# A transformer-block kernel: the norm's shift and scale in two parts, two projections split by rows between their slabs, routing steps six then four

## The chip, the core and the metric

One core of a Trainium2 chip runs the whole program. The time is device microseconds (us) of one execution; lower is better. Everything is float32. The engines are PE (TensorE), DVE (VectorE), ACT (ScalarE), POOL (GpSimd) and SP (SyncE, which here only issues transfers).

## What is computed

Two layers on 256 tokens of 1024 features. Only the first part of the first layer is touched by the change, and the routing of its expert layer:

```python
mod = (silu(c) @ w_mod + b_mod)              # 1024 -> 6144
sh1, sc1, gt1, sh2, sc2, gt2 = split(mod, 6)
h = rmsnorm(x, ln_mix_g) * (1 + sc1) + sh1   # 256 x 1024
proj = h @ w_in                              # q, kc, vc, ks, vs, kw, vw, gates, 3 x conv
# attention (compressed, selected, window) and a short convolution, then
x = x + gt1 * (mixed @ w_out)
h2 = rmsnorm(x, ln_ffn_g) * (1 + sc2) + sh2
# 8 heads: scores against 2 x 128 keys, top 16 of each half, top 16 of the 256 sums
x = x + gt2 * sum(g * gelu(h2 . u[expert]) * v[expert])   # 128 experts a token
# then a second layer (block attention, gated delta rule, 3 branches)
```

## The kernel before

**Stages.** 0 to 182 us of the profile are the front: modulation, norm, projections, attention of the first 128 tokens, output projection, first routing. 182 to about 975 us are the expert loop: 128 steps `p`, each of two gathers (`fetch`, POOL, an indirect DMA of 128 rows of `in_puv`, 1 MB), two dot products (`dot`, DVE, L1722), weights (`weight`, ACT) and two accumulations (`accumulate`, PE, L1095). The rest of the attention, the routing of later heads and the second layer are laid between these steps by `loop_chores`. After it comes the end of the second layer.

**Slabs.** A weight matrix is read in slabs of 8 x 128 rows x 512 columns (2 MB, two transfers of 4 x 128 rows each: L2529). The table `SLABS` (L157) numbers them; `W` has four slots and slab `i` of the first 22 goes to slot `i % 4`. `load(i, *free)` in `sync` (L2524) waits for the event that frees the slot and issues; SP does its loads strictly in the order written (from L2540), so one waiting load holds all behind it. The slabs of the front:

- 0 to 3: the columns of `w_mod` for shift and scale of the first norm (`sh1` in 0 and 1, `sc1` in 2 and 3; each slab has 512 of the 1024 features);
- 4 (`S_Q`) queries, 7 (`S_KV`) compressed and selected keys and values, 9 (`S_KW`) window keys, values and gates, 11, 14, 16 (`S_CV`) the convolution's three projections;
- 5, 6, 8, 10, 12, 13, 15, 17 (`S_MOD`) the other eight slabs of `w_mod`, which DVE alone multiplies: `mods(m)`, by `weighted_rows` (L1399), eight DVE instructions of 128 x 512 that sum `w[k] * c[k]` over k;
- 18, 19 (`S_WO`) and 20, 21 (`S_WQ`): output projection and the queries of the routing.

**The first modulation.** For slabs 0 to 3 the work is shared: PE multiplies the first 256 columns (`mod_front`, L806, 8 matmuls, one output row, copied by ACT in `mod_row`), DVE sums the other 256 (`weighted_rows` into `half_buf`, 128 x 256). `columns` (L799) turns the rows into columns of `modc` by single-column matmuls. `mod1` adds the bias and makes `sc1`. Only then do `evacuate` on DVE (L1429; features k = 0, 1, 4, 5) and on ACT (L2159; k = 2, 3, 6, 7) write the normed, scaled, shifted `hT` from the transposes of `norm_T` (L820). `queries` and `keys_values` (matmuls by `feat`, L771, and `token`, L779) run over all eight k for each output tile.

**The order after it.** PE: `flip_bias` (L849), `window`, `conv_project(0, 0)`, `scores_mm(0)` (L937), `compress(0)`, `scores_mm(1)`, ..., `cmp_s1(0)` (L899), ..., `cmp_turn(0, 0)` (L921). DVE: `mods(0)`, `mods(1)`, `blocks` (L1441), `flip_bias` (L1448), `mods(2)`, `mods(3)`, `scores_add(0)` (L1459 and on), `weigh(0)`, `scores_add(1)`, `weigh(1)`, `mods(4)`, `mods(5)`, `compress_k`, `compress_v`, `mods(6)`, `cmp_s2(0)`, `cmp_s3(0)`, ... SP, around there: slab 12 after `mods(2)`, 14 after `mods(3)`, 16 after `mods(4)`, 15 after `conv_project(0, 1)`, 17 after `mods(5)`.

**The routing.** `route(a)` is a generator of small DVE steps: eight or more per head. `loop_chores` lets it advance by a fixed number of steps after each `p` (L495), besides what a gather needs at once:

```python
            while (a, (2 * m + g) // 16) not in idx:
                advance(routes, 1)
...
        advance(routes, 6 if p < 8 else 5 if p < 16 else 4 if p < 33 else 8)
```

`take_i` (L1705) writes the gather indices of two heads; those of heads 2 and 3 are needed from p = 16 on. A gather also needs a free buffer, and in these steps six are in use, so the gathers of `p` wait for the accumulations of `p - 3`.

## Time and profile before

| what | value |
|---|---|
| median of 3 runs | 1257.31 us (1254.69 to 1258.04) |
| the profiled execution | 1260.68 us, its span 1258.9 us |
| PE, DVE, ACT, POOL busy | 1078.0, 796.0, 456.8, 295.8 us |
| moved by DMA | 432.08 MB, mean 343 GB/s |
| granted PE clock, mean | 0.944 of full |

The span is what the profiler saw from first to last instruction; 1.8 us of the execution's own time lie outside. The page of the profile gives the span in 40 slices of 31.5 us; a timeline row is start, length, engine, source line, operation, output and inputs, shape, count, and in brackets the idle time before it with the engine and line that ended it. A matmul in float32 leaves two PE records, so x16 are 8 matmuls.

### The profile page before, as it was taken

The page shows a single profiled execution, that of the slowest core. Times are in us where ns is not written, and L with a number is a line of the kernel's source. Part 1 is how long each engine was busy: PE and PEld are TensorE (multiplying, and loading weights), DVE is VectorE, ACT ScalarE, POOL GpSimd, SP SyncE. Part 2 cuts the span into 40 slices and gives each one's busy share as a digit, 9 for nine tenths or more (in the row PEclk, how much of TensorE's full clock was granted, in tenths as well). Part 3 has the DMA queues.
Part 4 walks back from the last instruction along what each step waited for, and adds up shares of the span by engine and source line. Part 5 has one row for each costly group of instructions (what it writes and reads, how often), then busy time and mean ns, then how long its engine had stood idle before and what let it go on. Part 6 is the DMA issues. An engine that isn't in the chain of part 4 may idle for free.

```text
span 1258.9 us, 13841 instructions
## 1 busy us (share of the span) xinstructions
PE 1078.0 (86%) x5002; PEld 536.8 (43%) x5002; DVE 796.0 (63%) x1865; ACT 456.8 (36%) x1257; POOL 295.8 (23%) x261
## 2 busy tenths in 40 slices
PE   6998986977887676769988789968998998999998
PEld 2887572432343222313332344423443444565543
DVE  5567758887763999764457667576655477645201
ACT  1132127555342444443353343434334423332201
POOL 0000013434343344433323333332323000000000
PEclk9999987998898889989999899988999999999999
DMA  9987419999999999999999999999999975344573
GB/s 388 409 328 316 169 47 370 364 354 411 421 383 421 417 404 395 378 423 401 421 421 420 421 421 420 420 422 363 421 420 423 380 268 200 142 160 154 212 293 127
DMA packets 63487, 432.08 MB, mean 343 GB/s; under 512 B 6931, under 2 KB 10300, under 8 KB 11836
## 3 DMA queue, kind: packets, MB, share of 16 engines
q0 software_dynamic: 36864, 268.45, 52.4%
q1 hardware_dynamic: 26160, 161.76, 32.3%
q10 hardware_dynamic: 396, 0.99, 0.2%
q8 instruction: 39, 0.64, 0.2%
q14 instruction: 28, 0.23, 0.0%
HBM read 430.12 MB, written 1.06 MB: 343 GB/s over the span
## 4 chain that ended last, share of the span: by engine, by line
PE 51%; DVE 20%; DMA 19%; ACT 5%; issue 2%; POOL 1%; another core or an unknown queue 0%; SPq 0%; DVEq 0%
PE ps L1140 22%; DMA AR<-in_puv,idx 17%; PE ps L1095 10%; DVE AR L1722 7%; PE ps L771 4%; PE ps L1254 3%; PE ps L990 2%; DMA W<-in_w_mod 2%; PE ps L1121 1%; PE ps L806 1%; POOL AR L2513 1%; PE ps L1035 1%; ACT av L2258 1%; DVE RT L1694 1%; ACT acc L2137 1%
## 5 line engine op out<-in xcount | busy, mean ns | idle before, releaser
L2513 POOL DMA_INDIRECT AR<-in_puv,idx x256 | 295.5, 1154 | 675.4 <-PE ps L1095 433.1
L1095 PE MATMUL ps<-AR,acc 128*64 128x512 f32 x904 | 286.6, 672 | 100.2 <-ACT acc L2137 98.4
L1722 DVE CUSTOM_DVE_ANT_0 AR<-AR,mixT 128x1024 f32<-128x1024 f32 x128 | 153.5, 1222 | 69.6 <-DMA AR<-in_puv,idx 69.3
L1140 PE MATMUL ps<-W,AR 128*128 128x512 f32 x416 | 189.2, 598 | 0.7 <-ACT AR L2137 0.7
L1095 PEld LDWEIGHTS ps<-AR,acc 128*64 128x64 f32 x904 | 71.8, 146 | 263.8 <-ACT acc L2137 169.5
L1722 DVE CUSTOM_DVE_ANT_0 AR<-AR,tok 128x1024 f32<-128x1024 f32 x128 | 153.0, 1220 | 48.4 <-DMA AR<-in_puv,idx 48.3
L1140 PE MATMUL ps<-W,hT 128*128 128x512 f32 x320 | 158.4, 626 | 6.5 <-DVE PT L2029 5.2
L2256 ACT ACTIVATE av<-av 128x1 f32<-128x1 f32 x256 | 51.3, 200 | 286.7 <-DVE av L1722 286.1
L1140 PEld LDWEIGHTS ps<-W,AR 128*128 128x128 f32 x416 | 76.1, 191 | 78.8 <-issue 76.7
L1140 PEld LDWEIGHTS ps<-W,hT 128*128 128x128 f32 x320 | 58.1, 198 | 83.3 <-issue 74.7
L2137 ACT ACTIVATE acc<-fold,av 128x64 f32<-128x64 f32 x226 | 78.6, 348 | 7.4
L2258 ACT ACTIVATE av<-av,gwp 128x1 f32<-128x1 f32 x256 | 75.4, 294 | 8.3
L771 PE MATMUL ps<-hT,W 128*128 128x256 f32 x320 | 71.4, 383 | 0.0
L771 PEld LDWEIGHTS ps<-hT,W 128*128 128x128 f32 x320 | 61.0, 192 | 8.7 <-issue 0.5
L1095 PE MATMUL ps<-AR,mixT 128*64 128x512 f32 x120 | 47.1, 732 | 17.4 <-ACT mixT L2137 16.8
L2137 ACT ACTIVATE AR<-ps 128x512 f32<-128x512 f32 (+3 forms) x26 | 14.4, 560 | 100.9 <-PE ps L771 43.2
L2007 DVE TENSOR_TENSOR RT<-RT,ps 64x256 f32<-64x256 f32 (+1 forms) x63 | 27.2, 431 | 34.9 <-PE ps L1254 31.4
L2137 ACT ACTIVATE mixT<-ps 128x512 f32<-128x512 f32 (+2 forms) x19 | 9.2, 485 | 81.6 <-PE ps L1140 26.8
L2256 ACT ACT_TABLE_LOAD x26 | 33.4, 1283 | 0.5
L1035 PEld LDWEIGHTS ps<-hT,W 128*128 128x128 f32 x224 | 27.6, 202 | 9.6 <-issue 9.5
L1140 PE MATMUL ps<-W,tok 128*128 128x512 f32 x64 | 31.3, 625 | 0.0
L1035 PE MATMUL ps<-hT,W 128*128 128x128 f32 x224 | 30.0, 291 | 0.0
(459 smaller groups left out, 1311.2 us busy)
## 6 DMA issues: line engine op xcount, KB each, us to landing
W<-in_w_in SPq DMA_DIRECT2D x90, 1024.0 KB, 11.5
W<-in_w_mod SPq DMA_DIRECT2D x24, 1024.0 KB, 16.0
W<-in_wba SPq DMA_DIRECT2D x8, 1024.0 KB
W<-in_wbb SPq DMA_DIRECT2D x8, 1024.0 KB
W<-in_wo SPq DMA_DIRECT2D x8, 1024.0 KB
W<-in_w_out SPq DMA_DIRECT2D x4, 1024.0 KB, 5.7
W<-in_wq SPq DMA_DIRECT2D x4, 1024.0 KB
AR<-in_puv,idx POOLq DMA_INDIRECT x256
```

The source lines that it names most:

```text
L771: t = mm(b[:, o:o + S], slab(i)[:, k, c:c + P], src[:, k, :], start=(k == 0), stop=(k == 7))
L990: t = mm(b[:, :], mixT[:, k, a * P:a * P + P], slab(S_WO[n])[:, k, :], start=(k == 0), stop=(k == 7))
L1035: t = mm(b[:, j * P:j * P + P], slab(S_WQ[m // 2])[:, k, c:c + P], hT[:, k, a * P:a * P + P], start=(k == 0), stop=(k == 7))
L1095: t = mm(of(("E", a, c))[64 * g:64 * g + 64, :], dg_at((2 * p + g) % NDG, late), GB[:, places[g], D + c * 512:D + c * 512 + 512], start=(m ...
L1140: t = mm(b[:, :], src[:, k, :], slab(i)[:, k, :], start=(k == 0), stop=(k == 7))
L1254: t = mm(b[c, q * P + c.start:q * P + c.stop], lhsT[c, q, c], rhs[c, q, c], start=True, stop=True)
L1722: ttr(GB[:, n, 0:D], GB[:, n, 0:D], H2[a][g], 1.0, 0.0, MUL, ADD, av[:, a, c:c + 1]).then_inc(*ve.sig("dot", p, g))
L2007: t = tt(o[c, :, c], o[c, :, c], src[c, :, c], SUB)
L2137: act(dst, src, ACT.Copy, **how).then_inc(*ac.sig(*name))
L2256: t = link(act(w, w, ACT.Gelu_apprx_tanh))
L2258: t = link(act(w, w, ACT.Copy, scale=gwp[:, a, c:c + 1]))
L2513: eng.indirect_dma_start(GB[:, n, :], None, puv, bass.IndirectOffsetOnAxis(ap=idx[:, a, c:c + 1], axis=0)).then_inc(*gp.dma(f"g{n}", "gat" ...
```

## The change

**Two parts.** The four slabs of the first modulation are loaded in the order shift and scale of the features k = 0 to 3 (slots 0, 1), then of k = 4 to 7. `mod_first` on PE makes the first part (slabs 0 and 1 shared between PE and DVE as before). Slabs 2 and 3 are summed by DVE alone, over all 512 columns; `mod_second` on PE only turns them into columns. `mod1(part)` and `evacuate` run once for each part.

**Lower and upper rows.** `queries_lo` and `keys_values_lo` multiply rows k = 0 to 3 of the queries' slab and of the keys' and values' slab as soon as the first half of `hT` is there; `queries` and `keys_values` add k = 4 to 7 later, into the same banks. So that several tiles can share a bank, `open_banks` first writes zeros to four banks by a one-row matmul of 512 columns each. `c` (both v) now shares one bank, `ks` and `vs` another, and `c_mm` and `ksv_mm` are signalled once.

**Slabs.** Slabs 4 and 9 get places of their own in `AR`; slab 4 and 7 are loaded half by half; the others get new slots (`SLOT`). On SP, slab 12 now waits for `mods(3)` and 13 for `mods(2)`, since 12 shares slot 0 with slab 10. On DVE `mods(1)` stands behind `flip_bias`, and `mods(3)` between `weigh(0)` and `scores_add(1)`; both sums of squares of x stand ahead of both norms.

**Routing.** Six steps after each p below 17, four below 33, instead of six below 8, five below 16, four below 33.

DVE, from the last `mods` ahead of the first scores to the second scores (`W` is the slab ring, s_w0 to s_w3 the load events of its slots; a row of 128x512 from `W` and its `x7` are one `mods`; the rows from L1459 or L1505 to the next such row are `scores_add` and `weigh`). Before:

```order
L1403 TENSOR_SCALAR RT<-W,st 128x512 [waits s_w0]
L1406 SCALAR_TENSOR_TENSOR RT<-W,st,RT 128x512 [waits s_dve] x7
L1403 TENSOR_SCALAR rowb<-W,st 128x512 [waits s_w2]
L1406 SCALAR_TENSOR_TENSOR rowb<-W,st,rowb 128x512 [waits s_dve] x7
L1459 TENSOR_TENSOR tok2<-ps1,acc 128x512 [waits s_pe_attn]
L1462 TENSOR_REDUCE sm2<-tok2 128x4 [waits s_ve_attn]
L1468 RECIPROCAL sm2<-sm2 128x4 [waits s_ac_attn]
L1470 TENSOR_TENSOR sm2<-sm2,AR 128x4 [waits s_dve]
L1472 TENSOR_TENSOR tok2<-tok2,sm2 128x512 [waits s_dve]
L1459 TENSOR_TENSOR tok2<-ps3,acc 128x512 [waits s_pe_attn]
```

The same place with the change:

```order
L1447 TENSOR_SCALAR RT<-W,st 128x512 [waits s_w1]
L1450 SCALAR_TENSOR_TENSOR RT<-W,st,RT 128x512 [waits s_dve] x7
L1505 TENSOR_TENSOR tok2<-ps2,acc 128x512 [waits s_pe_attn]
L1508 TENSOR_REDUCE sm2<-tok2 128x4 [waits s_ve_attn]
L1514 RECIPROCAL sm2<-sm2 128x4 [waits s_ac_attn]
L1516 TENSOR_TENSOR sm2<-sm2,AR 128x4 [waits s_dve]
L1518 TENSOR_TENSOR tok2<-tok2,sm2 128x512 [waits s_dve]
L1447 TENSOR_SCALAR rowb<-W,st 128x512 [waits s_w0]
L1450 SCALAR_TENSOR_TENSOR rowb<-W,st,rowb 128x512 [waits s_dve] x7
L1505 TENSOR_TENSOR tok2<-ps4,acc 128x512 [waits s_pe_attn]
```

`mods(3)` has moved from ahead of the first scores to between the first and the second, and reads slot 0.

PE, from the last transposes of the norm to the queries' upper rows, with the change (`ps1` holds the columns, `ps2` to `ps5` are the opened banks; s_wk_lo and s_wq_hi are halves of the slabs 7 and 4):

```order
L843 MATMUL ps0<-K,tok2 128x128 x4
L782 MATMUL ps4<-hT,W 128x256 [waits s_wk_lo]
L782 MATMUL ps4<-hT,W 128x256 x7
L782 MATMUL ps5<-hT,W 128x256 x4
L790 MATMUL ps5<-W,hT 128x128 x8
L810 MATMUL ps1<-K,hT 128x1 [waits s_ve_cond]
L810 MATMUL ps1<-K,hT 128x1 x3
L810 MATMUL ps1<-K,hT 128x1 [waits s_ve_cond]
L810 MATMUL ps1<-K,hT 128x1 x3
L782 MATMUL ps2<-hT,AR 128x256 [waits s_ve_h,s_wq_hi]
```

Before, all columns and all transposes stood ahead of one unbroken run of 56 matmuls of 256 columns and 16 of 128; now each projection is met twice, and the second set of columns stands between its halves.

The diff, cut to what the steps below use:

```diff
-    [("w_mod", n * 512, 512) for n in range(4)]
+    [("w_mod", n * 512, 512) for n in (0, 2, 1, 3)]
...
+SLOT = (0, 1, 2, 3, None, 1, 2, 0, 1, None, 0, 3, 0, 1, 2, 3, 0, 1, 2, 3, 0, 1)
+
+
 def slot_of(i):
-    return i % NSLOT if i < FRONT else RING[(i - FRONT) % 3]
+    return SLOT[i] if i < FRONT else RING[(i - FRONT) % 3]
...
-        advance(routes, 6 if p < 8 else 5 if p < 16 else 4 if p < 33 else 8)
+        advance(routes, 6 if p < 17 else 4 if p < 33 else 8)
...
+        own = {S_Q: ar(12288, 4096).rearrange("p (k n) -> p k n", k=8), S_KW: ar(5952, 2240).rearrange("p (k n) -> p k n", k=8)}
+        MOD_AT = (0, 2, 1, 3)
+
         def slab(i):
-            return W[:, slot_of(i)]
+            return own[i] if i in own else W[:, slot_of(i)]
...
+            def feat(b, o, i, c, src, ready, k0=0, k1=8, whole=True, last=True):
+
+
+                pe.wait_ge(("w", i) if k1 == 8 else ("wl", i))
+                for k in range(k0, k1):
                     pe.wait_ge(*ready(k))
-                    t = mm(b[:, o:o + S], slab(i)[:, k, c:c + P], src[:, k, :], start=(k == 0), stop=(k == 7))
+                    t = mm(b[:, o:o + S], slab(i)[:, k, c:c + P], src[:, k, :], start=(k == 0 and whole), stop=(k == 7 and last))
...
+            def mod_first():
+
+                take("modc")
+                open_banks()
+                for n in range(2):
                     r, old = take(("modr", n), ("mod_row", n))
                     pe.wait_ge(*old, ("w", n), "cs")
                     for k in range(8):
                         t = mm(r[0:1, 0:256], cs[:, k:k + 1], slab(n)[:, k, 0:256], start=(k == 0), stop=(k == 7))
                     t.then_inc(*pe.sig("modr", n))
-                    if n:
-                        columns(n - 1)
-                columns(3).then_inc(*pe.sig("mod_cols"))
-
-            def norm_T(key, tiles, at, ready, frees):
-                for k2 in range(4):
+                mod_columns(0)
+                mod_columns(1).then_inc(*pe.sig("mod_cols", 0))
+
+            def mod_second():
+
+                mod_columns(2)
+                mod_columns(3).then_inc(*pe.sig("mod_cols", 1))
+                drop("modc", ("mod1", 1))
+
...
+            def open_banks():
+
+                for use in (("q", 0), ("q", 1), "c", "ksv"):
+                    b, old = take(use)
+                    pe.wait_ge(*old, "K", "zero")
+                    mm(b[:, :], ones[0:1, :], RT[0:1, 0:512], start=True, stop=False)
+
+            def queries_lo():
+                for j2 in range(2):
+                    for jj in range(2):
+                        feat(of(("q", j2)), jj * 256, S_Q, (2 * j2 + jj) * P, hT, h_k, k1=4, whole=False)
+
             def queries():
                 for j2 in range(2):
-                    b, old = take(("q", j2), ("qT", j2))
-                    pe.wait_ge(*old)
                     for jj in range(2):
-                        t = feat(b, jj * 256, S_Q, (2 * j2 + jj) * P, hT, h_k)
+                        t = feat(of(("q", j2)), jj * 256, S_Q, (2 * j2 + jj) * P, hT, h_k, k0=4, whole=False, last=(jj == 1))
                     t.then_inc(*pe.sig("q_mm", j2))
+                    drop(("q", j2), ("qT", j2))
...
+            def keys_values_lo():
+                for v in range(2):
+                    feat(of("c"), v * S, S_KV, v * P, hT, h_k, k1=4, whole=False)
+                feat(of("ksv"), 0, S_KV, 256, hT, h_k, k1=4, whole=False)
+                for a in range(2):
+                    token(of("ksv"), 256 + a * P, S_KV, 384, P, hT, a, h_k, k1=4, whole=False)
...
-            mod_front()
-            norm_T("h", (0, 1), lambda a, k: tok2[:, a, k * P:k * P + P], lambda a: ("xb", a), h)
+            mod_first()
+            norm_T("h", (0, 1), x_at, lambda a: ("xb", a), h, k2s=range(3))
+            queries_lo()
+            norm_T("h", (0, 1), x_at, lambda a: ("xb", a), h, k2s=(3,))
+            keys_values_lo()
+            mod_second()
             queries()
             keys_values()
             flip_bias()
...
+            def mod1(part):
+                f = slice(4 * part, 4 * part + 4)
+                ve.wait_ge(("mod_cols", part), "pc")
+                tt(quarters(modc[:, 0:16], part), quarters(of("modc")[:, 0:16], part), quarters(PV[:, V_BMOD:V_BMOD + 16], part),
+                   ADD).then_inc(*ve.sig("mod1", part))
+                ve.wait_ge(("mod1", part))
+                stt(sc1[:, f], sc1[:, f], 1.0, PV[:, V_LNM + 4 * part:V_LNM + 4 * part + 4], ADD, MUL).then_inc(*ve.sig("mod1_sc", part))
...
-            for n in range(4):
+            for n in range(2):
                 weighted_rows(n, half_buf(n)[:, 256:512], slice(256, 512), "mod_sum", n)
-            mod1()
-            evacuate("h", 0, S, sc1, sh1, ["mod1_sc"], h)
+            mod1(0)
+            evacuate("h", 0, S, sc1, sh1, [("mod1_sc", 0)], h, k2s=(0,))
+            for n in range(2, 4):
+                weighted_rows(n, half_buf(n), slice(0, 512), "mod_sum", n)
+            mod1(1)
+            evacuate("h", 0, S, sc1, sh1, [("mod1_sc", 1)], h, k2s=(2,))
             mods(0)
-            mods(1)
             blocks(0)
             blocks(1)
             flip_bias()
+            mods(1)
             mods(2)
-            mods(3)
             scores_add(0)
             weigh(0)
+            mods(3)
             scores_add(1)
             weigh(1)
...
-            for i in range(NSLOT):
-                load(i)
-            for i in range(NSLOT):
-                load(4 + i, ("modr", i), ("mod_sum", i))
+            load(0)
+            load(1)
+            load_part(S_Q, 0, "wq_lo", "wl", S_Q)
+            load(2)
+            load(3)
+            sp.wait_ge(("modr", 0), ("mod_sum", 0))
+            load_part(S_KV, 0, "wk_lo", "wl", S_KV)
+            load_part(S_Q, 4, "wq_hi", "w", S_Q)
+            load_part(S_KV, 4, "w0", "w", S_KV)
+            load(5, ("modr", 1), ("mod_sum", 1))
+            dma(cw[:, :], cmpw).then_inc(*sp.dma("in_cw", "cw"))
             sp.wait_ge("scr")
...
-            dma(cw[:, :], cmpw).then_inc(*sp.dma("in_cw", "cw"))
-            load(9, ("mods", 0))
-            load(10, ("mods", 1))
-            load(8, ("q_mm", 1))
-            load(11, "vs_mm")
-            load(13, "vw_mm")
-            load(12, ("mods", 2))
-            load(14, ("mods", 3))
+            load(S_KW)
+            load(11, ("mod_sum", 3))
+            load(6, ("mod_sum", 2))
+            load(8, ("mods", 0))
+            load(10, "ksv_mm")
+            load(14, ("mods", 1))
+            load(13, ("mods", 2))
+            load(12, ("mods", 3))
```

## Rows read from the trace of the kernel before

**Rows 1.** The page, part 2: GB/s moved in each of 40 slices

```profile
GB/s 388 409 328 316 169 47 370 364 354 411 421 383 421 417 404 395 378 423 401 421 421 420 421 421 420 420 422 363 421 420 423 380 268 200 142 160 154 212 293 127
```

**Rows 2.** The chain that ended last, in order of time, the front (start, us)

```profile
98.96 10.83 DMA W<-in_w_mod
...
118.15 1.87 PE ps L921 x8
```

**Rows 3.** Timeline of PE, 12 to 84 us

```profile
13.15 9.89 PE L806 MATMUL ps<-W,st 128*1 128x256 f32 x32 [3.63 <-DMA W<-in_w_mod]
...
24.04 3.61 PE L806 MATMUL ps<-W,st 128*1 128x256 f32 x16
...
32.20 2.20 PE L799 MATMUL ps<-K,hT 1*128 1x1 f32 x16
34.27 1.94 PE L820 MATMUL ps<-K,tok 128*128 128x128 f32 x16
36.04 24.34 PE L771 MATMUL ps<-hT,W 128*128 128x256 f32 x112
...
63.79 3.60 PE L849 MATMUL ps<-mixT,K 128*128 128x512 f32 x8
...
81.81 1.16 PE L937 MATMUL ps<-AR 64*128 64x128 f32 x8
```

**Rows 4.** DMA issues before 130 us: size, and us from issue to landing

```profile
K<-in_cst ACTq DMA_DIRECT2D x1, 809.0 KB, 10.3
```

**Rows 5.** Timeline of DVE, 12 to 118 us

```profile
28.86 3.61 DVE L1406 SCALAR_TENSOR_TENSOR hT<-W,st,hT 128x256 f32<-128x256 f32 x7
...
34.94 1.90 DVE L1429 TENSOR_SCALAR hT<-ps,modc 128x256 f32<-128x256 f32 x4
39.42 0.49 DVE L1403 TENSOR_SCALAR RT<-W,st 128x512 f32<-128x512 f32 x1 [2.58 <-DMA W<-in_w_mod]
...
74.58 5.48 DVE L1406 SCALAR_TENSOR_TENSOR rowb<-W,st,rowb 128x512 f32<-128x512 f32 x7
83.00 0.69 DVE L1459 TENSOR_TENSOR tok<-ps,acc 128x512 f32<-128x512 f32 x1 [2.95 <-PE ps L937]
...
87.15 0.69 DVE L1459 TENSOR_TENSOR tok<-ps,acc 128x512 f32<-128x512 f32 x1
...
92.13 5.48 DVE L1406 SCALAR_TENSOR_TENSOR rowb<-W,st,rowb 128x512 f32<-128x512 f32 x7
...
109.81 0.49 DVE L1403 TENSOR_SCALAR AR<-W,st 128x512 f32<-128x512 f32 x1 [5.96 <-DMA W<-in_w_mod]
```

**Rows 6.** Timeline of SP's issues, 96 to 142 us

```profile
97.64 0.80 SPq L2529 DMA_DIRECT2D W<-in_w_in  x2
...
128.08 12.02 SPq L2529 DMA_DIRECT2D W<-in_wq  x4
```

**Rows 7.** Windows: PE, PEld, DVE, ACT, POOL busy, PE clock, DMA share, GB/s

```profile
134.00:136.00 2.00, 2.00 (x11) 1.77 (x10) 1.73 (x7) 1.29 (x8) 0.00 (x0) 1.00 0.28 119
```

**Rows 8.** Windows, PE alone: busy, clock, DMA share, GB/s

```profile
118.00:120.00 2.00, 1.85 (x9) 0.50 1.01 426
```

**Rows 9.** Timeline of POOL (the gathers), 255 to 290 us

```profile
267.83 0.94 POOL L2513 DMA_INDIRECT AR<-in_puv,idx  x1 [5.63 <-PE ps L1095]
...
276.73 0.94 POOL L2513 DMA_INDIRECT AR<-in_puv,idx  x1 [6.32 <-DVE RT L1618]
```

**Rows 10.** Timeline of DVE, 255 to 290 us

```profile
273.28 0.28 DVE L1614 MATCH_REPLACE8 rowb<-RT,ps 128x128 f32<-128x128 f32 x1
...
275.77 0.19 DVE L1705 CAST idx<-ps 128x32 uint32<-128x32 f32 x1
```

**Rows 11.** Windows as in Rows 7, around that gather

```profile
274.00:276.00 2.00, 0.51 (x4) 0.20 (x3) 2.00 (x6) 0.59 (x1) 0.00 (x0) 1.00 0.78 315
276.00:278.00 2.00, 1.99 (x18) 1.95 (x19) 1.93 (x10) 0.59 (x1) 0.97 (x2) 1.00 0.24 94
278.00:280.00 2.00, 0.73 (x5) 0.41 (x4) 2.00 (x7) 1.46 (x6) 1.45 (x1) 1.00 0.79 217
```

More of the change, by code:

```diff
@@ L764, in of, with token @@
                 return ps[bank[use]]
-            def feat(b, o, i, c, src, ready):
-                pe.wait_ge(("w", i))
-                for k in range(8):
+            def feat(b, o, i, c, src, ready, k0=0, k1=8, whole=True, last=True):
+                pe.wait_ge(("w", i) if k1 == 8 else ("wl", i))
+                for k in range(k0, k1):
                     pe.wait_ge(*ready(k))
-                    t = mm(b[:, o:o + S], slab(i)[:, k, c:c + P], src[:, k, :], start=(k == 0), stop=(k == 7))
+                    t = mm(b[:, o:o + S], slab(i)[:, k, c:c + P], src[:, k, :], start=(k == 0 and whole), stop=(k == 7 and last))
                 return t
-            def token(b, o, i, c, n, src, a, ready):
-                pe.wait_ge(("w", i))
-                for k in range(8):
+            def token(b, o, i, c, n, src, a, ready, k0=0, k1=8, whole=True, last=True):
+                pe.wait_ge(("w", i) if k1 == 8 else ("wl", i))
+                for k in range(k0, k1):
                     pe.wait_ge(*ready(k))
-                    t = mm(b[:, o:o + n], src[:, k, a * P:a * P + P], slab(i)[:, k, c:c + n], start=(k == 0), stop=(k == 7))
+                    t = mm(b[:, o:o + n], src[:, k, a * P:a * P + P], slab(i)[:, k, c:c + n], start=(k == 0 and whole), stop=(k == 7 and last))
                 return t
@@ L789, in bias_row, with mod_columns @@
                 mm(b[0:8, 0:383], tab, oh_sb, start=True, stop=True).then_inc(*pe.sig("bias_mm"))
-            def mod_front():
-                cols, _ = take("modc", ("mod1",))
-                def columns(n):
-                    for j in range(4):
-                        c = slice(j * P, j * P + P)
-                        pe.wait_ge("K", ("mod_row", n) if j < 2 else ("mod_sum", n))
-                        lhsT, one = (half_buf(n)[0:1, c], ones[0:1, 0:1]) if j < 2 else (half_buf(n)[:, c], ones[:, 0:1])
-                        t = mm(cols[:, 4 * n + j:4 * n + j + 1], lhsT, one, start=True, stop=True)
-                    return t
-                for n in range(4):
+            def mod_columns(n):
+                cols, at = of("modc"), 4 * MOD_AT[n]
+                for j in range(4):
+                    c = slice(j * P, j * P + P)
+                    row = n < 2 and j < 2
+                    pe.wait_ge("K", ("mod_row", n) if row else ("mod_sum", n))
+                    lhsT, one = (half_buf(n)[0:1, c], ones[0:1, 0:1]) if row else (half_buf(n)[:, c], ones[:, 0:1])
+                    t = mm(cols[:, at + j:at + j + 1], lhsT, one, start=True, stop=True)
+                return t
+            def mod_first():
+                take("modc")
+                open_banks()
+                for n in range(2):
                     r, old = take(("modr", n), ("mod_row", n))
@@ L807, in mod_front, with x_at, norm_T @@
                     t.then_inc(*pe.sig("modr", n))
[L808 to L813 removed]
+                mod_columns(0)
[4 more added lines that the diff above has]
+                drop("modc", ("mod1", 1))
+            def x_at(a, k):
+                return tok2[:, a, k * P:k * P + P]
+            def norm_T(key, tiles, at, ready, frees, k2s=range(4)):
+                for k2 in k2s:
                     b, old = take((key, k2), frees(2 * k2 + 1))
@@ L835, in keys_values @@
-                    feat(b, 0, S_KV, v * P, hT, h_k).then_inc(*pe.sig("c_mm", v))
-                b, old = take("ks", ("ksT",))
-                pe.wait_ge(*old)
-                feat(b, 0, S_KV, 256, hT, h_k).then_inc(*pe.sig("ks_mm"))
-                b, old = take("vs", ("vs",))
-                pe.wait_ge(*old)
+                    t = feat(of("c"), v * S, S_KV, v * P, hT, h_k, k0=4, whole=False, last=(v == 1))
+                t.then_inc(*pe.sig("c_mm"))
+                drop("c", ("blk", 0, 1), ("blk", 1, 1))
@@ L1432, in blocks @@
             def blocks(v):
[L1434 removed]
+                ve.wait_ge("c_mm", "cw")
                 for o in range(2):
@@ L2450, in scalar @@
                 x_root(a)
-            for n in range(4):
+            for n in range(2):
                 mod_row(n)
-            evacuate("h", (1, 3), 0, S, sc1, sh1, ["mod1_sc"], h)
+            for part in range(2):
+                evacuate("h", (1 + 2 * part,), 0, S, sc1, sh1, [("mod1_sc", part)], h)
             for j2 in range(2):
```

50 lines of the change are left out of this document (25 added, 25 removed).

## The prediction, made before the changed kernel was run

> **What bounds the kernel now.** I read the slices first [rows 1]: the DMA queue is full (about 421 GB/s) for most of the expert loop, so the loop ends when it began plus its bytes, plus the holes in the stream. It cannot begin before the front ends, and the front has no other load to overlap: 169 and 47 GB/s in the slices ahead of the loop. A microsecond taken from the front, or a hole closed in the loop, is therefore a microsecond of the whole; the end after the loop, bound by PE, only moves. Second, the chain of waits in the front [rows 2]: a wait of 10.83 us for a slab of `w_mod` that ends at 109.8, and a start of PE at 118.15 (`cmp_turn`). Third, the timelines of PE and DVE, to see who leads where [rows 3, 5]. From 36.04 to 63.79 PE runs the projections of queries, keys and values without a pause, and DVE waits for it until the first scores at 83.00. From 83.00 on it is DVE that leads: first scores, second scores from 87.15, `mods(4)` to 97.6; then SP can ask for slabs 16 and 15 [rows 6], 15 comes at 109.81, `mods(6)` runs, and PE, out of work, waits for what DVE does after it. So the front's length is decided by **when `mods(4)` ends**, not by when PE is done with its projections.
>
> **The change, PE.** Removed: two of four rows of the first modulation, 3.6 us each [rows 3], 7.2 us. Added: four zeroing matmuls of 512 columns. Nothing shows one with a single input row; the nearest is the flip, 3.60 / 4 = 0.90 us; below, nothing, above, 0.9 at half clock, 1.8. I take 0.90, 3.6 in all. They wait for `K`, which lands 10.3 us after its issue at about 2.2 [rows 4], so they run from 12.5 to 16.1, and the first row ends at 19.7. The second row was held by its slab to 23.04 - 3.6 = 19.4 before, so it now ends at 23.3: the cover of the zeroing is that wait, and 0.3 us of it shows. Then columns (2.2) to 25.5, 12 of 16 transposes (1.5) to 27.0, 16 matmuls for the queries' lower rows (24.34 / 56 = 0.435 each, 7.0) to 33.9, four transposes (0.5) to 34.4.
>
> The lower half of slab 7 is in time: slab 5 came at 39.42 before, behind 13.6 MB in all [rows 5]; this half stands behind 2.1 MB less, 5.0 us at 421 GB/s, so 34.4. All of queries, keys and values took 27.75 us, a half 13.9; the lower rows of keys and values end at 34.4 + 6.9 = 41.3. The second columns follow, if DVE has its sums: slab 2 comes near 27.0 by the same count, two sums of 5.97 us (0.49 + 5.48) end at 39.0. So 2.3 us of slack. Columns to 43.5, then bias, scale and the first evacuation, 1.0 us (from 34.4, the end of the columns, to 35.4, a quarter into the evacuations [rows 3, 5]), upper rows 13.9: **58.5 instead of 63.79, 5.3 us earlier**. The splitting itself costs this one gap; evacuations in two groups cost nothing else, since lower-row matmuls cover the first. From there to the first scores PE's work is unchanged (19.2 us) and its slabs are early, so these come at 77.7 instead of 83.00. DVE has done `mods(2)` by then (copies of the flips from 59.6 to 62.9, two `mods` to 74.8). The earlier squares of x bring DVE 1.4 us earlier to slab 0, and it then waits for slab 1: nothing.
>
> **The change, DVE and SP.** Added on DVE: half a slab in each of two sums, 2 x (5.97 - 3.96) = 4.0 us, hidden in its waits for PE. From the first scores on nothing is hidden. First scores and weights take 4.15 us (83.00 to 87.15) to 81.9. Now `mods(3)` follows, 5.95, to 87.8; until now it was done before the first scores, in DVE's slack. Second scores take 4.4 (87.15 to 91.6) to 92.2. `mods(4)` needs slab 12, and slab 12 now waits for slot 0 until `mods(3)` ends. SP asks 0.1 us later; a single slab into an empty queue is not timed by itself here, so: the slab asked for at 128.08 was through 0.6 us into the slice at 134, since 119 GB/s for 2 us are 0.57 us at 421 [rows 6, 7]: 6.5 us. Bounds: 5.0, the bytes alone, and 12.2, what two slabs took from 97.6 to 109.8. With 6.5, `mods(4)` starts at 94.4 and ends at 100.3, **2.7 us later than before**. Behind the waiting load stand rows, 16, 15 and 17; slab 15 takes the same 12.2 us after `mods(4)`, `mods(6)` starts at 112.5, PE's `cmp_turn` at 120.9, and every later step of the front is 2.7 us late. PE in between: `cmp_s1` waits for `compress_k` behind `mods(5)`, 100.3 + 5.95 = 106.3; the work from it to `cmp_turn` is below ten microseconds (it fitted between the end of `mods(5)`, 103.5, and 113.7) and ends at 116.6, in time. So of PE's 5.3 us nothing arrives, and the front costs **+2.7** (bounds: -5.3, if DVE is not late; +8.4, with the 12.2 us).
>
> Here the clock matters. After idleness (the wait that ended at 118.15) PE's granted clock stood at 0.50, the lower level of 1.2 GHz, through the slice 118 to 120 [rows 8]; some 3.4 us at half speed cost 1.7. Now PE is idle from about 97 to 106.5; with 1.7 lost it reaches 118.3, still 2.6 us ahead of 120.9, so I add nothing. The Trainium skill ("TensorE: Matmul & The Clock Gate", HAM oscillation) says that a matmul engine left waiting between bursts falls back to the low clock and starts the next burst cold, which speaks against a change that adds such a gap. The row agrees; by the rule alone, without the look at who ends last, the sum would be 1.7 us higher.
>
> **The change, routing.** Ten more steps by p = 16, each between 0.28 and 0.7 us, mostly near 0.36 (one of the short kind: 0.28 [rows 10]). They bring `take_i` of heads 2 and 3 from p = 14 to p = 13. Before, its indices were ready at 275.8, and the gathers of p = 16, issued 5 us after their forerunners in a steady stream, came 8.9 us after them (267.83, 276.73) [rows 9, 10]; the stream had a hole, (106 + 327 + 204) / 421 x 2 = 3.0 us [rows 11]. One p is about 5 us, two megabyte gathers at 421 GB/s, so the indices would be ready near 271, and the buffers 5 us after the forerunners, near 273. I take the whole hole, **-3.0**. Bounds: -5, if the slower stretch before it fills too, and +4, ten steps on the critical engine.
>
> **Sum:** 1260.68 + 2.7 - 3.0 = 1260.4 us in terms of the profiled execution, which is 3.4 above the median; that is -0.3, so 1257.0 as a median. Under 0.3% (3.8 us) counts as no change, about what a measurement of this kernel can tell.
>
> **Rivals.**
> - **PE's lead arrives.** If `mods(4)` ends no later than PE's pace, because slab 12 comes at once, or DVE gets its first scores before 75.0, the front gains up to 5.3: 1257.3 - 5.3 - 3.0 = 1249.0. For it: PE is the largest part of the chain in the front, and all its slabs come earlier. Against: the order on DVE, where 6 us of sum and a reload stand between two scores. 0.30.
> - **DVE cannot take the ten steps.** In the loop from p = 8 to 16 DVE is the busiest engine (all of the slice 274 to 276 [rows 11]). If the steps fall on it where no gather is waited for, dots and so buffers come later, and p = 16's gathers gain nothing: about 8 of the steps at 0.36, +2.9, with the front's +2.7: 1262.9. It decides from the point where the dots of p = 13 start later than before, measured from the loop's start. Against: DVE still waits for gathers in p = 9 to 11. 0.24.
> - **The hole is not the indices'.** If the buffers are free only at 276, the routing brings nothing: 1257.3 + 2.7 = 1260.0. 0.08.
> - **Half clock after the second columns.** Single columns and a 1 us wait, 3.2 us in all, stand before the upper rows; if the clock falls there, 1.7 us of PE's lead go, and they pass on undiminished, since DVE waits for PE's scores: 1258.7. Before, 2.2 us of columns went by at full clock. 0.06.
> - The forecast itself: 0.32.
>
> **Numbers.** Forecast 1257.0. Faster 0.30 (the first rival), slower 0.24 (the second), the same 0.46. The range holds all but the edges: from the first rival's 1249.0 to the second's 1262.9 and a little, 1263.5.
>
> **What would show it.** In the profile after: the flips (L849's successor) near 58.5; first scores near 77.7; `mods(4)` starting after a wait for DMA near 94 and ending near 100; PE idle some 9 us before `cmp_s1`; PE's `cmp_turn` near 121; first gather near 185.3 instead of 182.6; the gathers of p = 16 about 5.5 us after those of p = 15. I am wrong if `mods(4)` ends before 97.6, or if the loop from first gather to last takes longer than before.

## The result: slower by half a per cent, and the profile after

The changed kernel takes **1262.41 us** (median of 12 runs, 1259.55 to 1265.78), the kernel before 1257.01 in the runs beside it (12 runs, 1254.37 to 1260.30): a ratio of **1.0049**, interval 1.0036 to 1.0061. By that ratio it is +6.2 us (the two medians lie 5.4 apart): slower, inside the range, and on the side to which I had given 0.24, though not by the rival that stood there. The profiled execution took 1265.78 us, span 1264.0; it is 3.4 above its median, as that of before was.

| place (start, us) | before | forecast | after |
|---|---|---|---|
| second row of the first modulation ends | 23.04 | 23.3 | 29.4 |
| flips | 63.79 | 58.5 | 67.34 |
| first scores on DVE | 83.00 | 77.7 | 86.56 |
| `mods(4)` ends | 97.6 | 100.3 | 110.3 |
| `mods(6)` starts | 109.81 | 112.5 | 123.86 |
| `cmp_turn` on PE | 118.15 | 120.9 | 132.20 |
| first gather | 182.58 | 185.3 | 195.09 |
| last gather | 970.47 | | 978.19 |

So the front is 12.5 us longer (195.09 - 182.58), and the gathers' loop, which carries the new pace, 4.8 shorter (783.10 against 787.89). Both are differences of two single executions: over all the kernels below this loop takes 786.0 to 787.9 us with the old pace (three executions) and 779.4 to 786.3 with the new one (eleven). Line numbers of after: L851 is `open_banks`, L821 the rows of the first modulation, L810 the columns, L843 the transposes, L782 and L790 `feat` and `token`, L887 the flips, L937 `cmp_s1`, L959 `cmp_turn`; on DVE L1447 and L1450 the weighted rows, L1475 `evacuate`, L1505 the scores.

Timeline of PE after, from 12 us, the counterpart of [rows 3]:

```profile
12.32 7.19 PE L851 MATMUL ps<-RT,K 1*128 1x512 f32 x8 [3.01 <-DMA K<-in_cst]
19.44 9.97 PE L821 MATMUL ps<-W,st 128*1 128x256 f32 x32
29.34 2.20 PE L810 MATMUL ps<-K,hT 1*128 1x1 f32 x16
...
48.74 1.84 PE L810 MATMUL ps<-K,hT 128*128 128x1 f32 x16
51.71 8.83 PE L782 MATMUL ps<-hT,AR 128*128 128x256 f32 x32 [1.13 <-DVE hT L1475]
...
67.34 3.60 PE L887 MATMUL ps<-mixT,K 128*128 128x512 f32 x8
```

The four zeroing matmuls are eight records and take 7.19 us; the four flips, also eight records of 512 columns, take 3.60. Behind them the two rows take 9.97, as they did before (9.89 [rows 3]), so of the 7.19 us only the 0.83 before 13.15 are covered: the rows end at 29.4 in place of 23.04, 6.4 us late. The upper rows start after a wait of 1.13 us and take 8.83 for what is 7.07 at full clock.

The windows of PE around both places, after (columns as in [rows 7]; the first number behind the bounds is the length):

```profile
12.00:18.00 6.00, 5.68 (x7) 2.49 (x8) 4.61 (x12) 1.35 (x3) 0.00 (x0) 1.00 1.01 421
18.00:24.00 6.00, 6.00 (x13) 1.35 (x12) 4.63 (x10) 0.00 (x0) 0.00 (x0) 1.00 1.02 426
24.00:30.00 6.00, 6.00 (x27) 2.46 (x26) 0.00 (x0) 0.75 (x2) 0.00 (x0) 1.00 1.01 422
...
34.00:36.00 2.00, 2.00 (x7) 1.59 (x7) 1.89 (x4) 0.00 (x0) 0.00 (x0) 0.60 0.97 406
...
54.00:56.00 2.00, 2.00 (x6) 1.61 (x5) 1.91 (x3) 0.00 (x0) 0.00 (x0) 0.50 0.98 410
```

In the last one, 0.50, PE is at 1.2 GHz behind the second columns; in the one before it, 0.60, behind the first. The first window shows no such number although PE works at half pace in it; more on that below.

Timeline of DVE after, from the first scores on, the counterpart of [rows 5]:

```profile
86.56 0.69 DVE L1505 TENSOR_TENSOR tok<-ps,acc 128x512 f32<-128x512 f32 x1 [2.95 <-PE ps L975]
...
91.22 5.47 DVE L1450 SCALAR_TENSOR_TENSOR rowb<-W,st,rowb 128x512 f32<-128x512 f32 x7
96.61 0.68 DVE L1505 TENSOR_TENSOR tok<-ps,acc 128x512 f32<-128x512 f32 x1
...
104.35 0.49 DVE L1447 TENSOR_SCALAR rowb<-W,st 128x512 f32<-128x512 f32 x1 [3.51 <-DMA W<-in_w_mod]
...
123.86 0.49 DVE L1447 TENSOR_SCALAR AR<-W,st 128x512 f32<-128x512 f32 x1 [7.27 <-DMA W<-in_w_mod]
```

and SP's requests beside it:

```profile
96.72 0.81 SPq L2580 DMA_DIRECT2D W<-in_w_mod  x2
...
110.38 0.80 SPq L2580 DMA_DIRECT2D W<-in_w_in  x2
111.22 5.86 SPq L2580 DMA_DIRECT2D W<-in_w_mod  x4
```

Read the two together: `mods(3)` (91.2) ends at 96.6; SP, which waits for it, asks for slab 12 at 96.72; it is there 7.6 us later, after DVE has waited 3.51 us for it. `mods(4)` ends at 110.3, SP asks for 16 and then 15, and 15 comes 13.5 us later, after another 7.27 us of waiting. The delay of the front is thus 3.56 us at the first scores, 12.7 at `mods(4)` (+5.95 of `mods(3)`, +3.5 of the wait, -0.3 elsewhere), 14.05 at `mods(6)` and at `cmp_turn`, and 12.5 at the first gather, since `cmp_turn` and what follows it run at full clock this time: its eight records in 1.03 us against 1.87 [rows 2], the 32 behind them in 7.07 against 7.81.

```profile
116.49 2.72 PE L937 MATMUL ps<-kcT,AR 64*128 64x7 f32 x16 [9.73 <-DVE vc L1527]
...
132.20 1.03 PE L959 MATMUL ps<-K,AR 128*7 128x128 f32 x8 [2.00 <-DVE AR L1557]
```

The gathers of p = 15 and 16 after, the counterpart of [rows 9]; counted from the first gather they come at 83.49 and 90.18 us, before at 85.25 and 94.15:

```profile
278.58 0.94 POOL L2566 DMA_INDIRECT AR<-in_puv,idx  x1 [3.92 <-PE ps L1133]
...
285.27 0.94 POOL L2566 DMA_INDIRECT AR<-in_puv,idx  x1 [4.50 <-DVE RT L1664]
```

### The profile page after: what moved, and what is told of

The parts are those of the page before. It is cut to its first block, busy times and chain, and to the rows that moved or that the text cites. A ratio compares the mean times of both kernels' runs of the same rounds, so it can differ in the third digit from the quotient of the medians.

```text
span 1264.0 us, 13796 instructions
## 1 busy us (share of the span) xinstructions
PE 1069.8 (85%) x4978; PEld 535.5 (42%) x4978; DVE 800.5 (63%) x1868; ACT 454.0 (36%) x1254; POOL 287.8 (23%) x261
## 4 chain that ended last, share of the span: by engine, by line
PE 48%; DMA 22%; DVE 19%; ACT 7%; issue 2%; POOL 1%; SPq 0%; ACTq 0%; DVEq 0%; POOLq 0%
DMA AR<-in_puv,idx 20%; PE ps L1178 19%; PE ps L1133 9%; DVE AR L1768 7%; PE ps L782 4%; PE ps L1028 2%; PE ps L1292 2%; PE ps L1073 2%; DMA W<-in_w_mod 2%; POOL AR L2566 1%; PE ps L1159 1%; DVE rowb L1450 1%; DMA K<-in_cst 1%; PE ps L821 1%; ACT av L2310 1%
## 5 line engine op out<-in xcount | busy, mean ns | idle before, releaser
L2566 POOL DMA_INDIRECT AR<-in_puv,idx x256 | 287.5, 1123 | 690.8 <-PE ps L1133 437.6
L1133 PE MATMUL ps<-AR,acc 128*64 128x512 f32 x904 | 279.2, 661 | 107.7 <-ACT acc L2190 106.5
L782 PE MATMUL ps<-hT,W 128*128 128x256 f32 x240 | 54.6, 386 | 0.0
L782 PEld LDWEIGHTS ps<-hT,W 128*128 128x128 f32 x240 | 46.0, 194 | 6.4
L1073 PEld LDWEIGHTS ps<-hT,W 128*128 128x128 f32 x224 | 27.6, 202 | 9.5 <-issue 8.6
```

Of the source, the lines that this page charges most:

```text
L782: t = mm(b[:, o:o + S], slab(i)[:, k, c:c + P], src[:, k, :], start=(k == 0 and whole), stop=(k == 7 and last))
L1073: t = mm(b[:, j * P:j * P + P], slab(S_WQ[m // 2])[:, k, c:c + P], hT[:, k, a * P:a * P + P], start=(k == 0), stop=(k == 7))
L1133: t = mm(of(("E", a, c))[64 * g:64 * g + 64, :], dg_at((2 * p + g) % NDG, late), GB[:, places[g], D + c * 512:D + c * 512 + 512], start=(m ...
L2566: eng.indirect_dma_start(GB[:, n, :], None, puv, bass.IndirectOffsetOnAxis(ap=idx[:, a, c:c + 1], axis=0)).then_inc(*gp.dma(f"g{n}", "gat" ...
```

## Experiments

Twelve kernels ran. Theory: the front loses at two places that the change makes (zeroing matmuls ahead of the rows; `mods(3)` with slab 12 behind it between the scores), the pace wins. The rivals: the pace is what costs; or the split of the projections costs by itself (the half clock, the second evacuation); or a front's delay does not reach the end at all. "Gather" is the start of the first one in the profiled execution; its spans differ by 1 to 3 us between executions of one kernel, the ratios are what counts.

**The pace alone, on the kernel before.**

```diff
-        advance(routes, 6 if p < 8 else 5 if p < 16 else 4 if p < 33 else 8)
+        advance(routes, 6 if p < 17 else 4 if p < 33 else 8)
```

> The kernel before with the new routing pace alone (six steps up to p = 16). Theory A (the front is what lost, the routing gained): the front is unchanged, first gather at 182.6 us; the gathers of p = 16 follow those of p = 15 by 5 to 7 us instead of 8.9, and the last gather and the end come 3 to 5 us earlier: ratio to before 0.996 to 0.998. Theory B (the routing steps load DVE and the 5 us that came back in the loop are a late start that the loop absorbs by itself): ratio 1.000 to 1.003.

Measured: 1253.73 us, ratio 0.9967 (0.9948 to 0.9986). The pace wins 4.1 us (1.8 to 6.5 by the interval). The gathers of p = 15 and 16 stand 6.69 us apart instead of 8.90, as in the changed kernel:

```profile
264.78 0.94 POOL L2513 DMA_INDIRECT AR<-in_puv,idx  x1 [3.93 <-PE ps L1095]
...
271.47 0.94 POOL L2513 DMA_INDIRECT AR<-in_puv,idx  x1 [4.51 <-DVE RT L1618]
```

The rival in which DVE cannot take the ten steps has fallen.

**The old pace in the changed kernel** (the same two lines, the other way round).

> The changed kernel with the old routing pace. Theory A: front as in the changed kernel (first gather at 195.1), the hole ahead of the gathers of p = 16 is back, and the time is 3 to 5 us above the changed kernel: ratio to before 1.007 to 1.009. Theory B: the loop gives back its 5 us with the old pace too: ratio 1.003 to 1.005.

Measured: 1266.95 us, ratio 1.0072 (1.0046 to 1.0099), gather 191.92. The front alone costs 9 us, and 1.0072 x 0.9967 = 1.0039, within the interval of the change: the two halves add. Its flips start at 64.29, not 67.34, although up to there it is the changed kernel, instruction for instruction. So three of after's 3.6 us at the flips come and go between executions (rows of 8.46 us here against 9.97, and a clock of 1.00 from 32 to 36 us against 0.54 and 0.60). Of the five executions with this beginning three went the one way (9.93 to 10.00 us, about 0.57 from 32 to 36 us) and two the other (8.38 and 8.46, 1.00). The costs below stand in both.

**The zeroing matmuls first.** They need `K` only for a row of ones; times a row of zeros from DVE it is zero too.

```diff
             take("modc")
-            open_banks()
...
-                pe.wait_ge(*old, "K", "zero")
-                mm(b[:, :], ones[0:1, :], RT[0:1, 0:512], start=True, stop=False)
+                pe.wait_ge(*old, "zero")
+                mm(b[:, :], RT[0:1, 0:128], RT[0:1, 0:512], start=True, stop=False)
...
+            open_banks()
             bias_row()
```

> The changed kernel with the four zeroing matmuls as PE's first work, from a row of zeros that DVE writes (so they wait neither for the constants nor stand ahead of the first modulation's rows). Theory A (the 6.4 us by which PE's second row ends later are the zeroing, 7.2 us, and what it does to the rows behind it): the second row ends near 23 instead of 29.3, the flips begin near 61, the first scores on DVE near 80 instead of 86.6, mods(4) ends near 104 instead of 110.3, first gather near 189: ratio to before 0.999 to 1.001. Rival: PE's lateness is carried to nothing, since DVE and the reload of slot 0 decide: first scores earlier but mods(4) still near 110, ratio 1.004 to 1.006.

```profile
1.56 7.19 PE L850 MATMUL ps<-RT 1*128 1x512 f32 x8 [1.56 <-DVE RT L2103]
```

Measured: 1261.51 us, ratio 1.0025 (1.0007 to 1.0043), against 1.0049 for the change. The same eight records take the same 7.19 us, now ahead of everything; the upper rows start at 44.59 (forecast for the change: 44.6), the flips at 59.99, the first scores at 79.20. Here the projections' part of the forecast comes true to 1.5 us, and the kernel is still no faster than before: `mods(4)` ends at 103.2, gather 187.18. The ratio came out worse than expected (at most 1.001), though gather and `mods(4)` came early by 2 and 1 us. Its interval still overlaps that of the change (1.0036 to 1.0061); what is clear is the trace.

**`mods(3)` back ahead of the first scores.**

```diff
+            mods(3)
             scores_add(0)
             weigh(0)
-            mods(3)
             scores_add(1)
```

> The changed kernel with mods(3) back ahead of the first scores on DVE, nothing else. Theory A (slot 0's chain of mods(3), reload of slab 12, mods(4) decides behind the first scores): mods(3) runs 83.7 to 89.6, the first scores come 3 us later than in the changed kernel (89.6), yet slab 12 comes at about 97 and mods(4) ends near 104 instead of 110.3; first gather near 189, ratio to before 0.999 to 1.001. Rival (the first scores' time is what passes on): everything 3 us later, ratio 1.007.

Measured: 1258.93 us, ratio 1.0011 (0.9992 to 1.0031), gather 185.97. `mods(4)` now starts without any wait (95.03, right behind the second scores) and ends at 100.9, though the first scores come at 86.42. Its flips start at 64.33, as with the old pace (64.29), where `mods(4)` ended at 107.2: the moved line gains 6.3 us there. That is also why all came 3 us before the times that I had expected, which I had counted from after. One exchanged line on DVE is worth 0.4%, and this interval lies clear of the change's.

**The second columns covered**: `keys_values_lo` cut in two, its last 12 matmuls (24 records) behind `mod_second`.

```diff
             keys_values_lo()
             mod_second()
+            keys_values_lo2()
             queries()
```

> The changed kernel with the second modulation columns put between the first half of the c product and the first half of the keys and values, so that TensorE has 5.3 us of products between the columns and the upper rows while VectorE adds the bias and evacuates. If the 1.13 us hole and the half clock in front of the upper rows cost what the profile of the change shows (rows of 8.6 to 8.8 us against 7.1), the upper rows run in 7.2 us without a wait, the flips start 2 to 3 us earlier than in the changed kernel (61.3 to 65.3), and the first gather with them; ratio to before 1.002 to 1.004. Rival: what holds mods(4) and mods(6) is the modulation slabs and VectorE, then nothing of it reaches the first gather, which stays within 1 us of the change's, and the ratio at 1.005.

```profile
48.78 1.95 PE L790 MATMUL ps<-W,hT 128*128 128x128 f32 x16
50.56 7.07 PE L782 MATMUL ps<-hT,AR 128*128 128x256 f32 x32
```

Measured: 1261.23 us, ratio 1.0037 (1.0021 to 1.0052), gather 191.28. The wait of 1.13 us and the half clock are both gone, 7.07 against 8.83, and the flips start at 64.44, 2.9 us before after's; the rows took 9.93, as there. What it wins in the time, 0.12%, cannot be told from the change's own interval.

**The zeroing once more, with PE busy before it.** The same four matmuls a second time, adding zeros behind the lower keys and values.

> The changed kernel with the four matmuls that add the row of zeros issued a second time (onto the sums, so that nothing changes in them), behind the lower keys and values where TensorE has been busy for over 10 us. Price by the cold engine: eight records of 0.45 us, 3.6 us. Price by the form (one input row, 512 columns): eight records of 0.9 us, 7.2 us here too. For the end of the span 0 to +3 us.

```profile
49.22 3.70 PE L1350 MATMUL ps<-RT,K 1*128 1x512 f32 x8
52.85 3.39 PE L810 MATMUL ps<-K,hT 128*128 128x1 f32 x16
```

The windows around them:

```profile
50.00:52.00 2.00, 2.00 (x6) 0.84 (x5) 0.00 (x0) 0.00 (x0) 0.00 (x0) 1.00 1.06 427
52.00:54.00 2.00, 2.00 (x10) 1.24 (x8) 0.00 (x0) 0.00 (x0) 0.00 (x0) 0.77 1.03 426
54.00:56.00 2.00, 2.00 (x11) 2.00 (x11) 0.00 (x0) 0.00 (x0) 0.00 (x0) 0.50 1.00 418
```

Measured: 3.70 us for the eight, 0.46 each; the first eight, at 12.68, took 7.19 in the same execution. One input row costs what 128 cost, and the price at the start is that of the engine's state. The execution took 1272.99 us (one run), more than the +3 that I had allowed: its flips start at 74.25, since the columns and the upper rows behind the added matmuls ran slow as well (3.39 us for what takes 1.84, 10.08 for what takes 7.07). The granted clock was 1.00 through the added matmuls and fell to 0.50 right behind them, at about 53 us, although PE had not paused.

**Slab 15 asked for before slab 16**, on the kernel before, with the new pace. Slab 15 waits for a product that PE ends at 95.1 us in the kernel before, but it stands behind 16, which waits for `mods(4)`, there to 97.6 [rows 6]. Exchanged, it is asked for 3 us sooner and without 16's 2 MB ahead of it.

```diff
-            load(16, ("mods", 4))
             load(15, ("cv_mm", 0, 1))
+            load(16, ("mods", 4))
```

> The kernel before with the new routing pace, and with SyncE's two requests exchanged (slab 15, which waits for a product of the conv step, ahead of slab 16, which waits for mods(4)). If the front is set by slab 15 being asked for behind mods(4), mods(6) starts near 104 in place of 109.8, cmp_turn near 112.3, the first gather near 176.5, and the ratio is 0.992 to 0.994 (pace alone gave 0.9967). Rival: the slot of slab 15 is not free earlier, or the front's microseconds don't reach the end; then the ratio stays at 0.9967.

```profile
103.81 0.17 DVE L1476 COPY kcT<-ps 128x15 f32<-128x15 f32 x1
104.16 0.47 DVE L1403 TENSOR_SCALAR AR<-W,st 128x512 f32<-128x512 f32 x1
```

Measured: **1247.55 us**, ratio **0.9933** (0.9919 to 0.9948), gather 175.94: faster than both kernels. `mods(6)` follows `mods(5)` with no wait, where it waited 5.96 us [rows 5]; `cmp_turn` starts at 113.95, 1.6 us later than expected, because PE still runs a convolution product when DVE is ready.

**The exchange alone, old pace.**

> The kernel before with SyncE's exchange alone, old pace. If pace and exchange add, the ratio is 0.9933 / 0.9967 = 0.9966 (0.9945 to 0.9985), cmp_turn near 114 and the first gather near 177. Rival: the exchange pays only with the new pace (or the other way round); ratio 0.999 to 1.001 with the first gather at 177 all the same.

Measured: 1252.40 us, ratio 0.9960 (0.9945 to 0.9975), gather 176.49. Exchange and pace add.

**All four mends in the changed kernel** (zeroing first, `mods(3)` ahead, cover, exchange).

> The changed kernel with the zeroing matmuls first, mods(3) ahead of the first scores, the second columns covered, and SyncE's exchange. If the losses are those four and they add: rows end at 22, flips at 57 to 58, first scores at 76 to 77, mods(4) ends at 99 to 101, mods(6) starts behind it without a wait of over 2 us (100 to 104), cmp_turn at 109 to 112, first gather at 173 to 176; ratio 0.990 to 0.993. Rival: earlier work in the front collides with the slabs' transfers and the gain stops at the kernel before with the new pace, 0.997.

```profile
103.00 2.72 PE L938 MATMUL ps<-kcT,AR 64*128 64x7 f32 x16 [5.55 <-DVE vc L1530]
...
108.47 8.31 PE L782 MATMUL ps<-hT,W 128*128 128x256 f32 x32
116.61 1.04 PE L960 MATMUL ps<-K,AR 128*7 128x128 f32 x8
```

Measured: 1248.61 us, ratio 0.9938 (0.9924 to 0.9951), gather 178.59. Flips 58.05 and first scores 76.07 on PE, as expected (DVE, which now does `mods(3)` ahead of them, takes them up at 80.82); `mods(6)` at 103.04, as expected; but `cmp_turn` at 116.61, not 109 to 112, so gather and ratio miss what I expected. PE now comes last: it waits 5.55 us for DVE, runs `cmp_s1` at half pace (2.72 us against 1.50 in the exchange's kernel) and then 8.3 us of convolution before it. A lead of 6 us on PE is turned into idleness, and the idleness into a low clock. This is the rule that I had weighed (the Trainium skill, "TensorE: Matmul & The Clock Gate", HAM oscillation: a matmul engine left waiting between bursts starts the next one at the low clock); it decides only here, where PE and not DVE ends last. DVE was ready for `cmp_turn` at 111.2. From `cmp_s1` to `cmp_turn` PE took 13.6 us (103.00 to 116.61), the same work in the exchange's kernel 9.8 (104.13 to 113.95): 3.8 of the 5.4 us by which PE is late are the low clock.

That kernel, which keeps the old front, stands at 0.9933 (0.9919 to 0.9948), this one at 0.9938 (0.9924 to 0.9951), and its first gather comes 2.7 us later. With its losses taken out, the front in two parts is not shown to be worth anything.

**The two losses only** (zeroing first, `mods(3)` ahead).

> The changed kernel with the two losses taken out together: the zeroing matmuls first, and mods(3) ahead of the first scores; SyncE's order and the rest as in the change. If these two are what the change lost, and what it wins in front of them is swallowed by the wait for slab 15 (12.2 to 13.6 us behind mods(4), as before), mods(4) starts at 91 to 92 and ends at 97 to 98, mods(6) starts at 109.5 to 111, cmp_turn 117.5 to 119.5, first gather 180.5 to 182.5, and the ratio is that of the pace alone, 0.9955 to 0.998. Rival: the losses do not add, since the earlier front meets a slab that is late by itself; mods(4) starts at 94 or later, ratio 1.000.

Measured: 1254.58 us, ratio 0.9971 (0.9948 to 0.9994), gather 183.35, `cmp_turn` 118.64. That is the pace's 0.9967 and nothing else, although the flips start at 60.17, 3.6 us ahead of before. DVE takes it: with `mods(3)` ahead of the scores it is busy to 82.26, where before it stood waiting for PE to 83.00, so only 0.7 us of the 3.6 pass the first scores:

```profile
76.87 5.48 DVE L1450 SCALAR_TENSOR_TENSOR rowb<-W,st,rowb 128x512 f32<-128x512 f32 x7
82.26 0.68 DVE L1505 TENSOR_TENSOR tok<-ps,acc 128x512 f32<-128x512 f32 x1
...
110.30 0.49 DVE L1447 TENSOR_SCALAR AR<-W,st 128x512 f32<-128x512 f32 x1 [7.20 <-DMA W<-in_w_mod]
```

The rest goes in the wait for slab 15, which takes 13.4 us from the request here and took 12.2 before.

**A convolution product moved into PE's wait**, in the kernel with all four mends, and in the exchange's.

```diff
             compress_v()
+            conv_project(1, 1)
             cmp_s1(0)
...
             turn_p(1)
-            conv_project(1, 1)
             cmp_turn(0, 0)
```

> The fourfold mended kernel of the run before (0.9938), with the second half of the third-slab conv product moved on TensorE from in front of cmp_turn into the 5.6 us in which TensorE waits for VectorE. In that run VectorE was ready for cmp_turn at 111.2 us and TensorE reached it at 116.6, after an 8.3 us product begun at 108.5. If that product is the bound there, cmp_turn starts at 111 to 112, the first gather at 173 to 174.5, ratio 0.989 to 0.991. Rival: the score and turning matmuls behind it run cold or wait for the bank, cmp_turn gains under 2 us, ratio 0.992 to 0.995.

Measured: 1251.49 us, ratio 0.9947 (0.9924 to 0.9970), gather 178.02, no better than without the move. The rival holds in the ratio and in part in its reason. The first half of `cmp_turn` starts at 110.23, 6.4 us sooner, but it runs at half pace (four records in 1.01 us, where eight took 1.04 without the move), and the second half waits for ACT:

```profile
110.23 1.01 PE L960 MATMUL ps<-K,AR 128*7 128x128 f32 x4 [2.47 <-DVE AR L1560]
114.10 1.02 PE L960 MATMUL ps<-K,AR 128*7 128x128 f32 x4 [2.86 <-ACT AR L2193]
```

> The kernel before with the new pace, SyncE's exchange and the same move of the conv product. VectorE was ready for cmp_turn at 112.3 there and TensorE reached it at 113.95, so the move is worth 1.6 us at most, if cmp_s1, which now comes behind a 7.1 us product begun at 97, is not made later by it (TensorE was free at 103.6, so it is ready at 104 either way, about). First gather 174.3 to 176.5, ratio 0.992 to 0.994; with the run before this tells whether the two-part front is worth anything once its losses are out.

Measured: 1255.61 us, ratio 0.9976 (0.9954 to 0.9997), gather 183.75: worse than without the move, whose ratio was 0.9933. My expectation had the product begin at 97; it begins at 104.38, behind another that fills the time from 96.96. `cmp_s1` slips from 104.13 to 111.49 and DVE, which needs its result behind `mods(6)`, is 3 us later (the `L1496` row at 113.64 instead of 110.63); the second half of `cmp_turn` waits for ACT here too and starts at 119.36. PE waits 0.54 us ahead of `cmp_s1` in that kernel, too short a hole for a product of 7 us.

## Why the prediction was wrong, step by step

- **"I take 0.90, 3.6 in all"** is the first step that failed. A zeroing matmul took 1.80 us, exactly my upper bound, 7.19 in all, because PE was at its slow pace (0.90 us per record here, 0.46 later). Nor did these 7.19 us of work end the slow pace: the rows right behind them still took 9.97 (8.38 to 10.03 in all fourteen executions, with or without zeroing ahead; 7.2 at the pace of the next 16 records [rows 3]). I ranked the bounds by the nearest row, the flips, which run in mid-kernel. The row that should have decided stood in [rows 3]: the first 32 records of the rows take 9.89 us and the next 16 take 3.61, so PE was slow there too and the slab was not what held it.
- **"0.3 us of it shows"** fell with it. I took the second row to be waiting for slab 1, so that the first 3.6 us were covered. After a 7 us delay the rows still take 9.97: the wait was PE's slowness, which moved along. The first columns end at 31.5, forecast 25.5. With the zeroing moved to the front the upper rows start at 44.59, forecast 44.6, so the rest of this sum was sound.
- **The rival "half clock after the second columns"**, given 0.06, happened in every execution without the cover (8.59 to 8.83, and 10.08 with the zeroing repeated, against 7.07), and costs 1.7 us as I had worked it out. In the forecast I had left it out since 2.2 us of columns had gone by at full clock before. That was one execution: the clock fell behind the first columns, with no wait there, in after, and in the exchange's kernel with the moved product, which has the old front (0.63 and 0.51 from 34 to 38 us).
- **"2.7 us later than before"**: the mechanism was right, the order of events is what I described (`mods(3)` between the scores, slab 12 behind it, then slabs 16 and 15), and it seems the larger loss (1.0049 to 1.0011 when undone, against 1.0025 for the zeroing; these two intervals overlap). Its terms: 5.95 for `mods(3)`, exact; 7.6 us for slab 12 instead of 6.5 (I had it alone in the queue, and 0.6 MB of small loads are asked for right behind it); 13.5 for slab 15 instead of 12.2. With the first scores at 86.56 instead of 77.7, that makes 12.7 us at `mods(4)`. My lead on PE, 5.3, was the cushion that this loss was to be paid from, and it did not exist.
- **"The front costs +2.7"**: +12.5 in the profiled execution, +9 by the ratio with the old pace (5.8 to 12.4 by its interval), where my upper bound was +8.4. In the profiled execution with the old pace, whose first gather is 9.3 late, the terms are 2.7 as forecast, 5.8 for PE's lead that was not there, 1.0 for slab 12, 1.3 for slab 15, and 1.5 back from `cmp_turn` on at full clock. "A microsecond taken from the front, or a hole closed in the loop, is therefore a microsecond of the whole" held well: gathers at 176.5 and 191.9 with the old pace gave 0.9960 and 1.0072, 14.1 us for 15.4.
- **"Still 2.6 us ahead of 120.9, so I add nothing"**, for PE's idleness, held. It waits 9.73 us before `cmp_s1` and the following records run slow (2.72 us), but DVE ends last, with PE waiting 2.00 us for it.
- **"I take the whole hole, -3.0"**: -4.1 as a ratio alone, in the bounds. The gap at p = 16 closed by 2.2 us, to 6.7 and not 5.5; the other 1.8 had been won by p = 15, the slower stretch that I named as the reason for the lower bound. The mechanism was right, and its size within what the interval allows (1.8 to 6.5 us).
- The sum -0.3 was right in one term of two. +9 by the ratios for the front and -4.1 for the loop give +5, measured +6.2. That the time still lies inside the range is luck: its upper end was set by DVE taking the ten steps badly, which did not happen, and not by a front of +9.

## What to carry to other kernels

Price an added matmul at the place where it will run: early in a kernel, compare it with the records that are there now, and ask of a "wait for a slab" whether the records beside it run at their usual pace. And where two engines take turns in leading, an order that gives the other engine a lead is worth nothing until the one that ends last is moved: here 3.6 to 6 us won on PE brought nothing, and one exchange of two requests on the DMA queue brought 0.4%, because the one whose slot was free stood behind one that still waited.

## What the runs showed of the hardware

- **Half pace with a granted clock of 1.00.** In the window from 12 to 18 us the profile grants PE 1.00, and records of 512 columns take 0.90 us; from 49 us on in the kernel with the zeroing repeated, at the same 1.00, they take 0.46. From 18 to 24 us after, the same: 13 records, then 27 in the six microseconds behind them. So here the column does not show the slow pace at the start of an execution, and the records' own durations must be read. The Trainium skill ("TensorE: Matmul & The Clock Gate", part 1) has the array start at its lower clock, 1.2 GHz, until it has been at work; the two durations agree with it, the column does not.
- **Seven microseconds of one-row matmuls did not end the slow pace, and in mid-kernel the clock fell behind them.** After, the rows behind 7.19 us of zeroing took 9.97 us, as slow as those with no zeroing ahead of them (9.89 before). With the zeroing repeated at full clock, 3.70 us of it, the granted clock went from 1.00 to 0.50 at about 53 us without a pause on PE.
- **It is not the same in each execution of one front.** The 32 records of the two rows took 9.97 us after, 9.93 with the cover, 8.46 with the old pace, 8.38 with `mods(3)` ahead. Between 32 and 36 us the granted clock was 0.54 and 0.60 in one and 1.00 in another. What decides it stays open; no kernel here was made to find out.
- **A slab of 2 MB with nothing asked for just before it takes 7.6 to 8.7 us** from request to use (104.35 - 96.72 after, 97.29 - 89.37 with the zeroing first, 112.27 - 103.62 with the zeroing repeated), not the 6.5 that I had worked out. It is not alone in the queue: three small loads, 584 KB in all, are asked for within 2.1 us of it, which at 421 GB/s are 1.4 us by my estimate. How the rest varies stays open.
- **Slab 15 behind slab 16 takes 12.2 or 13.5 us** from the request: 12.2 before, 12.2 with the cover, 13.5 after, 13.4 in the kernel without the two losses. Nothing in the program differs between those two groups at that place; it stays open.
